# A fused decoder step on one core: two light experts ahead of the fullest one, and a last down matrix taken in column halves

## The reference

```python
y = jnp.zeros_like(xf)                       # xf: 288 x 2048
for e in range(N_EXPERTS):                   # 16 experts, w_gate, w_up: 2048 x 512, w_down: 512 x 2048
    h = jax.nn.silu(xf @ w_gate[e]) * (xf @ w_up[e])
    y = y + combine[:, e:e + 1] * (h @ w_down[e])
return h_in + y                              # the residual
```

## Time and profile before

| | |
|---|---|
| median of three runs | 1248.9 us (1248.38 to 1254.77) |
| the profiled execution | 1247.59 us |
| its span, first to last instruction | 1245.8 us |
| PE busy | 1161.0 us (93%) |
| DVE, ACT, POOL busy | 471.5, 192.9, 49.8 us |
| HBM read | 319.04 MB, mean 265 GB/s |
| chain that ended last | PE 79%, DVE 9%, DMA 6%, ACT 3% |

### The profile page before, as it was taken

One profiled execution on the slowest core, in us unless ns is written; L12 is line 12 of the kernel. 1 busy time (PEld: TensorE's weight loads), 2 busy tenths in 40 slices (PEclk: granted clock), 3 DMA queues, 4 the chain that ended last, 5 costly groups with the idle time before them and its releaser, 6 DMA issues.

```text
span 1245.8 us, 14135 instructions
## 1 busy us (share of the span) xinstructions
PE 1161.0 (93%) x5878; PEld 569.1 (46%) x5878; DVE 471.5 (38%) x962; ACT 192.9 (15%) x405; POOL 49.8 (4%) x64
## 2 busy tenths in 40 slices
PE   7999999899999998899999899999999999999665
PEld 5334343344444455577778565333333333334322
DVE  5000167079835645011112465233333333224232
ACT  2102232400122233100012422000000000000000
POOL 0002000000000003200000001000000000000000
PEclk9999999999999999899999998999999999889888
DMA  8836522345343338864445636999999999999996
GB/s 287 296 121 151 159 93 95 126 152 175 137 135 102 106 132 329 315 185 135 135 138 190 267 128 263 420 428 426 426 425 427 428 425 428 424 385 411 428 428 263
DMA packets 71229, 327.85 MB, mean 263 GB/s; under 512 B 14108, under 2 KB 17980, under 8 KB 54588
## 3 DMA queue, kind: packets, MB, share of 16 engines
q1 hardware_dynamic: 55152, 282.65, 58.1%
q0 software_dynamic: 8032, 37.23, 8.0%
q10 hardware_dynamic: 7980, 7.05, 2.3%
HBM read 319.04 MB, written 10.49 MB: 265 GB/s over the span
## 4 chain that ended last, share of the span: by engine, by line
PE 79%; DVE 9%; DMA 6%; ACT 3%; ACTq 2%; issue 1%; DVEq 0%; SPq 0%
PE PS L695 20%; PE PS L1002 15%; PE PS L1273 13%; PE PS L1355 7%; PE PS L1236 4%; PE PS L668 3%; PE PS L1280 3%; DMA ring<-in_w_up 2%; DMA nine<-in_w_up 2%; DVE X L2017 2%; DVE top L2016 2%; PE PS L813 1%; PE PS L1240 1%; PE PS L1348 1%; PE PS L986 1%
## 5 line engine op out<-in xcount | busy, mean ns | idle before, releaser
L695 PE MATMUL PS<-ring,NC 128*128 128x512 f32 x704 | 324.3, 606 | 1.6 <-issue 1.6
L695 PEld LDWEIGHTS PS<-ring,NC 128*128 128x128 f32 x704 | 129.9, 192 | 155.5 <-issue 153.9
L1002 PE MATMUL PS<-NC,ring 128*128 128x288 f32 x768 | 189.9, 407 | 1.6 <-DVE X L2174 0.5
L1002 PEld LDWEIGHTS PS<-NC,ring 128*128 128x128 f32 x768 | 144.6, 190 | 42.4 <-issue 2.1
L1273 PE MATMUL PS<-ring,NC 128*64 128x512 f32 x528 | 161.6, 598 | 1.4 <-DVE NC L2370 1.4
L2356 DVE TENSOR_TENSOR X<-X,PS 128x1024 f32<-128x1024 f32 x52 | 63.5, 1222 | 119.8 <-PE PS L1236 119.8
L1273 PEld LDWEIGHTS PS<-ring,NC 128*64 128x64 f32 x528 | 45.9, 136 | 89.3 <-issue 87.7
L1236 PE MATMUL PS<-XNN,NC 64*128 64x512 f32 x208 | 59.7, 650 | 1.1 <-DVE XNN L2403 0.6
L1864 ACT ACTIVATE NC<-PS,small 64x512 f32<-64x512 f32 x11 | 7.5, 682 | 312.7 <-PE PS L1273 271.4
L1280 PE MATMUL PS<-ring,mkT 128*32 128x256 f32 x384 | 34.9, 428 | 20.6 <-DMA ring<-in_w_up 12.9
L2174 DVE TENSOR_TENSOR X<-X,PS 128x288 f32<-128x288 f32 x16 | 7.3, 455 | 116.6 <-PE PS L1002 116.6
(11 more groups left out here) (446 smaller groups left out, 1208.7 us busy)
## 6 DMA issues: line engine op xcount, KB each, us to landing
ring<-in_w_gate SPq DMA_DIRECT2D x27, 2048.0 KB, 22.3
ring<-in_w_up SPq DMA_DIRECT2D x22, 2048.0 KB, 18.5
ring<-in_w_in SPq DMA_DIRECT2D x36, 1024.0 KB, 5.0
ring<-in_w_down SPq DMA_DIRECT2D x16, 2048.0 KB, 21.1
ring<-in_w_out SPq DMA_DIRECT2D x16, 1024.0 KB, 5.0
nine<-in_w_down SPq DMA_DIRECT2D x6, 2048.0 KB, 22.2
XNN<-in_w_up SPq DMA_DIRECT2D x5, 2048.0 KB, 19.3
NC<-in_w_gate SPq DMA_DIRECT2D x5, 2048.0 KB, 20.6
```

The lines of the kernel that those rows point to most:

```text
L695: last = mm(acc(n, t)[:, 0:width], lhs[:, kt, t * 128:(t + 1) * 128], slot(m)[:, k, 0:width], start=kt == 0, stop=kt == KT - 1)
L1002: last = mm(PS[:, j, 0:NT], slot(m)[:, k, 128 * j:128 * j + 128], src[:, kt, :], start=kt == 0, stop=kt == width * 4 - 1)
```

## The change

1. **Order.** `NEARLY = 2` light experts come at positions 10 and 11, in a block of their own (block 10); the fullest is at position 12, with block 11 and the first strip of block 12; the remaining three light ones follow at 13 (the second strip of block 12), 14 and 15 (block 13). The routing's arithmetic on DVE gets one more operation on 16 columns (`later`). The combine steps of a block stand at the position named in `COMBINED_IN`. The second layout of rows ahead of the fullest expert moves from position 9 to position 11.
2. **The last down matrix.** Lots 94 and 95 hold 1024 columns each with all 512 rows, in pieces of 4 KB. PE makes the products of one column half (`last_down`), then three pairs of combine products for it (`last_combine(0)`), then those of the other half. All four column strips and, in the combine, both row halves of TensorE work.
3. **Residuals on PE.** For the second prompt tile and the samples the residual is added in PSUM, by a product of the identity with `hx` (`residual`), so that ACT and DVE only copy.
4. **Stores.** Five instead of six: the first tile's halves from SP after DVE's additions, the second tile's halves from ACT after its copies, in pieces of 4 KB, and the samples in one.
5. **Idle products.** Six ahead of the last expert and three ahead of the second half of its gate and up steps; the residuals of the second tile's first half lie in between.

```diff
-PSTAR = NEXP - 1 - NLIGHT
-NBK = PSTAR + 1 + (NLIGHT + 1) // 2
+NEARLY = 2
+NFULL = NEXP - NLIGHT
+PSTAR = NFULL - 1 + NEARLY
+NBK = NFULL + (NLIGHT + 1) // 2
+BSTAR = PSTAR - NEARLY // 2
...
+        COMBINED_IN = {p: p - 1 for p in range(1, NFULL)}
+        COMBINED_IN.update({PSTAR: BSTAR - 1, PSTAR + 1: BSTAR, PSTAR + 2: BSTAR + 1})
...
+                    if e == NEXP - 1 and wv is down_v:
+                        out = out.rearrange("p (k n) -> p k n", k=4)
+                        source = down_cols[expert, :, :, 1024 * part:1024 * part + 1024]
...
+            def residual(out, t, col, opens=True):
+                rows = slice(0, ROWS[t])
+                mm(out, ident[rows, rows], hx[rows, t, col:col + 512], start=opens, stop=not opens)
+            def last_residuals(half, opens=True):
+                for x in range(2):
+                    residual(PS[:, 2 * half + x, :], 1, 1024 * half + 512 * x, opens)
+            def sample_residuals():
+                for c in range(4):
+                    residual(PS[32 * c:32 * c + 32, 4, :], 2, 512 * c)
+            def last_down(half, w):
+                for f in range(4):
+                    for c in range(4):
+                        last = mm(PS[32 * c:32 * c + 32, 5, 0:256], hTs[:, f, :], w[:, f, 256 * c:256 * c + 256],
+                                  start=f == 0, stop=f == 3)
+                last.then_inc(S("y_last"), 1)
+            def last_combine(half):
+                def product(out, tokens, x, opens):
+                    rows, k = slice(64 * x, 64 * x + 64), (NBK - 1) % 2
+                    return mm(out, slot_w[rows, k, tokens], ysb[rows, k, 512 * half:512 * half + 512], start=opens, stop=True)
+                if half:
+                    pe.wait_ge(S("y_ready"), 1)
+                for x in range(2):
+                    last = product(PS[:, 6 + x, :], slice(0, 128), x, True)
+                last.then_inc(S("last_comb"), 1)
+                for x in range(2):
+                    last = product(PS[:, 2 * half + x, :], slice(128, T), x, False)
+                last.then_inc(S("last_comb"), 1)
+                for x in range(2):
+                    c = 2 * half + x
+                    last = product(PS[32 * c:32 * c + 32, 4, :], slice(T, NT), x, False)
                 last.then_inc(S("last_comb"), 1)
...
+                def last_gap(s):
+                    if s == 0:
+                        last_residuals(0)
+                    if s == 2:
+                        keep_clock(3)
+                if p == NEXP - 1:
+                    pe.wait_ge(S("comb_free"), NCOMB_IN)
+                    keep_clock(6)
+                light_gate_up(rows_of(b), sub, lots_at(p), gap(p) if p < NEXP - 1 else last_gap)
...
+                if b + 1 == BSTAR and sub:
+                    block_rows_t(BSTAR + 1)
...
-            pe.wait_ge(S("y_strips"), 2 * (NLIGHT + 1))
-            for n, (t, x) in enumerate(LAST[:4]):
-                last_combine(t, x, 2 * n)
-            pe.wait_ge(S("y_ready"), 1)
             for half in range(2):
+                w = lots_at(NEXP - 1)(4 + half).rearrange("p (f n) -> p f n", f=4)
+                last_down(half, w)
+                if half == 0:
+                    sample_residuals()
+                    last_residuals(1)
+                pe.wait_ge(S("y_strips"), 2 * (NLIGHT + 1 + half))
+                last_combine(half)
...
+            def last_rows(half, c):
+                row, col = 64 * (c // 2) + STRIP, 512 * half + 256 * (c % 2)
+                return A(ysb[row:row + STRIP, (NBK - 1) % 2, col:col + 256], PS[32 * c:32 * c + 32, 5, 0:256], ACT.Copy)
+            for half in range(2):
+                act.wait_ge(S("y_last"), half + 1)
+                last_rows(half, 2)
+                last_rows(half, 3).then_inc(S("y_strips"), 1)
+                act.wait_ge(S("last_comb"), 3 * half + 2)
+                own(A(hx[:, 1, 1024 * half:1024 * half + 1024], PSF[:, 1024 * half:1024 * half + 1024], ACT.Copy))
+                act.dma_start(y_prompt[0, 128:T, 1024 * half:1024 * half + 1024], hx[:, 1, 1024 * half:1024 * half + 1024])\
+                    .then_inc(S("y_stored"), 16)
...
+            own(TS(later[:, 1:16], rnk[:, 1:16], float(PSTAR), float(CAP + STRIP), ALU.is_ge, ALU.mult))
...
+            for half in range(2):
+                dve.wait_ge(S("y_last"), half + 1)
+                last_rows(half, 0)
+                last_rows(half, 1).then_inc(S("y_strips"), 1)
+                dve.wait_ge(S("last_comb"), 3 * half + 1)
+                out = hx[:, 0, 1024 * half:1024 * half + 1024]
+                TT(out, out, PSF[:, 3072:4096], ALU.add).then_inc(S("y_ready"), 1)
+            dve.wait_ge(S("last_comb"), 6)
+            V.tensor_copy(y_last_s, PS[:, 4, :]).then_inc(S("y_ready"), 1)
```

More of the change, by code:

```diff
@@ L402, in decode_step @@
         tabF = small[:, 256:256 + 3 * NBLK]
-        rnk, s32, l32 = (small[:, 352 + 16 * i:368 + 16 * i] for i in range(3))
-        strips = small[:, 400:406].rearrange("p (s b) -> p s b", s=2)
+        rnk, s32, l32, later = (small[:, 352 + 16 * i:368 + 16 * i] for i in range(4))
+        strips = small[:, 416:424].rearrange("p (s b) -> p s b", s=2)
         over_rs = small[:, 490:491]
@@ L1334, in strip_down @@
                 return last
-            def last_combine(t, x, banks):
-                for half in range(2):
-                    rows = slice(64 * half, 64 * half + 64)
-                    last = mm(PS[0:ROWS[t], banks + half, :], slot_w[rows, (NBK - 1) % 2, t * 128:t * 128 + ROWS[t]],
-                              ysb[rows, (NBK - 1) % 2, 512 * x:512 * x + 512], start=True, stop=True)
+            def residual(out, t, col, opens=True):
[28 more added lines that the diff above has]
+                    last = product(PS[32 * c:32 * c + 32, 4, :], slice(T, NT), x, False)
                 last.then_inc(S("last_comb"), 1)
@@ L1879, in strip_rows @@
                 for x in range(2):
-                    last = A(ysb[64 + STRIP * sub:64 + STRIP * sub + STRIP, b % 2, 512 * x:512 * x + 512],
+                    row, col = (64 * x, 512) if b == NBK - 1 else (64, 512 * x)
+                    last = A(ysb[row + STRIP * sub:row + STRIP * sub + STRIP, b % 2, col:col + 512],
                              PS[64 + 32 * x:96 + 32 * x, bank, :], ACT.Copy)
                 last.then_inc(S("y_strips"), 1)
-            for p in range(PSTAR):
-                full_silu(p)
-                full_hidden(p, 3)
@@ L2240, in _ @@
             own(V.memset(route, 0.0))
-            own(V.memset(small[:, 352:400], 0.0))
+            own(V.memset(small[:, 352:416], 0.0))
             own(TT(sooner, bc(cc("iota_e")[:, 0:4], 1, [128, 4, 4]), bc(cc("iota_e")[:, 0:4], 2, [128, 4, 4]), ALU.is_lt))
```

247 lines of the change are left out of this document (125 added, 122 removed).

## The result

The changed kernel takes 1255.02 us (median of 15 runs, 1249.32 to 1265.82); the kernel before, on the same chip beside it, takes 1248.87. The ratio is 1.0057, with a 95% interval of 1.0040 to 1.0075. The change makes the kernel some 7 us slower. The forecast was 1246.0 us in a range of 1242.0 to 1251.5: wrong in sign and outside the range. The profiled execution is one of the quicker ones: 1252.97 us, with a span of 1251.1 against 1245.8 before.

A forecast was written before the change was run, and what follows sets the result against it. Transfers were taken to set the pace, save in a dent; its 3.2 us, less 0.3 for the tail and 0.1 for routing, gave span 1243.0 and median 1246.0 us against 1248.9, range 1242.0 to 1251.5.

The forecast's parts named there:

- The dent: Slow transfers from 1098 to 1129 us, caused by the fullest expert at position 10; the new order removes 3.2 us.
- The rival that the order does nothing: The lot queue starves again at the fullest expert's new place; 3.2 us not gained, 1249.2 against the median; chance 0.13.
- PE in time: Before the last expert's second half, PE is ready at 1215.2, with 2.1 us of slack before its lot lands.
- L: Landing of the last but two lot: 1220.5 us before, forecast to move to 1217.3.
- rival D: PE arrives late at the last expert, 6.4 us over the slack; 1252.4 against the median; chance 0.12.
- a last half at full clock: The last expert's second gate-and-up half takes 3.7 us instead of 5.4 if PE stays busy, gaining 1.7.
- The first down half and the residuals: In the tail, PE's first down half takes 1.9 us and the residuals 2.6, ending at 1228.3.
- a mechanism not seen: A little of the 0.07 chance given to a slower result, above 1255.1 us.
- The stores: At the kernel's end, 1.31 MB left to store instead of 2.36 MB; shorter stores save 3 us.
- The order on PE: Last down products wait for the first half's combine, until 1231.45, though their lot is in at 1227.5.
- B: Rival: dent worth 4.1 us, stores ending with the last issue, copies 0.4 less; 1243.2 against the median; chance 0.12.
- The chance of "faster": Chance 0.11 of a time below 1242.7 us.

The follow-up runs named there:

- no_idle: The changed kernel without its nine idle products; ratio 1.0065 to the kernel before.
- late_combine: Changed kernel with samples' store spread, both halves' down products before all six combine pairs, four and two idle products, 22 small ones; ratio 1.0055 to the kernel before.
- order_idle: The changed kernel's new order and nine idle products, with the end of the kernel before (old last down matrix, combine, stores); ratio 0.9980 to the kernel before.
- pad90: The changed kernel with 90 semaphore instructions added on PE ahead of the fullest expert; ratio 1.0062 to the kernel before.

## Why the prediction was wrong

**The dent.** Right in cause and place: no window under 420 GB/s, PE waiting for lots at positions 10 and 11, the fullest expert from 1117.82 to 1164.7 against the forecast 1119 to 1164. Its size was 2.4 us and not 3.2 on the mean of the profiles. The rival that the order does nothing is refuted by the trace, though the times of the order alone can't tell the gain from nothing.

**PE in time.** The forecast gave 2.1 us of slack; PE was 1.5 us late. Position 14 ended 12.2 us ahead of L (at 1203.3) instead of 15.2 (at 1202.1, with L at 1217.3), mostly since the fullest expert took 46.9 us and not 44.4: it began at the low clock, behind a wait of 7.07 us (its first eight instructions took 3.68 us, where rows 3 have 1.72). That is rival D, with 1.5 of its 6.4 us. The idle products cost 5.35 and 2.77 against 5.1 and 2.6; with PE late they only delay. no_idle, whose PE was in time, got the full clock without them. The forecast 1.7 us for a last half at full clock were gained (3.66 us).

**The first down half and the residuals**: the step that failed. It read "PE: first down half and residuals 1.9 + 2.6", and costed the way there at nothing. The way leads over a branch, and the change shifted the program behind it: 5.9 us more than forecast, of them 3.50 standing still until a piece of the program was in, and the rest low clock (3.63 for 29 instructions, 3.15 for the residuals). No row of before showed such a gap, but the forecast didn't name the branch as something whose price it couldn't know, and gave "a mechanism not seen" a few hundredths.

**The stores.** "Bytes behind that point: 1.31 MB" treated all stores alike. The samples' store has an outermost dimension of four, and ran on four engines: 2.3 to 2.8 us more. This stood in the diff, and the forecast read it as bytes alone.

**The order on PE**, which the forecast weighed against the change, was as forecast: the last down products stood behind the first half's combine and started at 1237.1, 11 us behind their lot. Undoing a part of that order gained under a us in late_combine, where the gap was still in the path.

**The range.** It took in D and B, each with its own term, and nothing for code that moves. The parts of PE's work that it listed were right to 0.3 us each, but for the fullest expert (2.5) and what ran behind the gap; the dent was off by 0.8 and the time behind the last copy by 2.2; the list was short. The chance of "faster" was also added up wrongly: a third of B's 0.12 and as much again is 0.08 and not 0.11.

No kernel here beats the kernel before beyond its interval; the nearest is order_idle with 0.9980 [0.9955, 1.0005]. The changed kernel without the overflow part and with the store spread, 1.0009 [0.9987, 1.0031], is level with it.

## What to carry to other kernels

Before costing an edit near the end of a kernel, look in the diff for two things that no duration shows: a branch over much code whose place in the program moves, and a DMA whose outermost dimension is small. In a trace, look for "issue" gaps in the middle of a row of equal products and for a DMA share that is a round fraction. And set work added to an engine that is nearly late against the slack that is left once the stages ahead run at the low clock: here 2.1 us of slack were forecast, and a first stretch at the low clock took more than that.

## What the runs showed that was not expected

- A stop of 1.9 to 4.0 us (0.62 in one kernel) on PE behind a branch over a few hundred instructions, whose place follows the program to the instruction (after 3, then after 21 matmul instructions, for 36 instructions less ahead), which ends 1.3 to 1.6 us behind a 16 KB packet on the instruction queue, and which is absent at some alignments.
- 90 semaphore instructions on PE took 11.4 us, 4.75 us of it on the path.
- The granted clock falls to 0.50 (the 1.2 GHz level) without such a gap too: in pad90 the first down half ran 2.91 us and the residuals 5.21 behind the hand-over of the hidden values, with no stop between. Why the clock falls in one execution and not in another of nearly the same work isn't settled here.
- The first column-half lot, in pieces of 4 KB, landed 5.05 us behind the lot before it in the changed kernel; the whole lots ahead of it were 4.90 apart.
- In six kernels with work added ahead of the fullest expert single lots landed 6.4 to 6.6 us behind the one before, though they had been issued 22 to 30 us earlier; why is open.
